# Latent attention: the order of evictions, query copies, weight splits and column sums in five queues

## The reference

```python
def rmsnorm(x, g):
    y = xf * lax.rsqrt(jnp.mean(xf * xf, axis=-1, keepdims=True) + EPS)
    return (y * g).astype(x.dtype)

mod = cond @ w_ada[i] + b_ada[i]                  # cond = silu(c); six vectors of 1024
sh1, sc1, gt1, sh2, sc2, gt2 = jnp.split(mod, 6, axis=-1)
h = rmsnorm(x, g_mix[i]) * (1.0 + sc1) + sh1

def mla(h, ...):
    cq = rmsnorm(h @ w_dq, g_q)                   # 1024 -> 384
    q = (cq @ w_uq).reshape(B, S, 8, 128 + 64)    # 8 heads; the last 64 are rotated
    ckv_kr = h @ w_dkv                            # 1024 -> 256 + 64
    ckv = rmsnorm(ckv_kr[..., :256], g_kv)
    k_rope = rope(ckv_kr[..., 256:], positions)
    kv = (ckv @ w_ukv).reshape(B, S, 8, 128 + 128)
    # causal softmax over 512 keys, p @ v, then o @ w_o
x = x + gt1 * mla(...)
...                                               # feed-forward, the second layer, the second block
```

## Time and profile before

| | us |
|---|---|
| median of 3 runs (2288.86 to 2292.99) | 2289.5 |
| the profiled execution | 2291.01 |
| its span | 2289.2 |
| TensorE busy in it | 2196.0 (96%) |
| VectorE, ScalarE, GpSimd busy | 1418.9, 964.0, 178.7 |

### The profile page before, as it was taken

How to read it: one execution, slowest core, us unless ns; L and a number is a source line. 1 busy time by engine, 2 the same in 40 slices (tenths; PEclk the granted TensorE clock), 3 DMA queues, 4 the chain that set the end, 5 groups by cost and what they waited for, 6 DMA issues and landing times.

```text
span 2289.2 us, 31979 instructions
## 1 busy us (share of the span) xinstructions
PE 2196.0 (96%) x13291; PEld 1940.5 (85%) x13291; DVE 1418.9 (62%) x2132; ACT 964.0 (42%) x1459; POOL 178.7 (8%) x155
## 2 busy tenths in 40 slices
PE   5988999999999899999989999999899999999998
PEld 3877888888898798898988999997778889899997
DVE  5676566556576667566446667654564545666674
ACT  3556343223256644463534444434443334443442
POOL 7210000000032100000010000002012001000000
PEclk8999999999999999999999999999999999999999
DMA  6442244555430212322312332333111332133230
GB/s 233 143 141 83 93 162 171 185 183 203 174 107 20 74 56 92 111 93 93 129 56 70 98 110 93 111 101 109 58 44 64 120 103 74 65 120 109 94 112 38
DMA packets 127734, 245.72 MB, mean 107 GB/s; under 512 B 4763, under 2 KB 36854, under 8 KB 127462
## 3 DMA queue, kind: packets, MB, share of 16 engines
q1 hardware_dynamic: 122832, 228.02, 29.5%
q0 software_dynamic: 4096, 15.28, 2.0%
q10 hardware_dynamic: 662, 0.37, 0.1%
HBM read 241.56 MB, written 2.10 MB: 106 GB/s over the span
## 4 chain that ended last, share of the span: by engine, by line
PE 81%; DVE 10%; ACT 4%; DMA 2%; issue 2%; POOL 0%; SPq 0%; DVEq 0%; ACTq 0%
PE PS L66 80%; DVE t L75 5%; ACT t L72 4%; DVE t L83 3%; DVE t L86 1%; DMA t<-in_ffn_w_dram 1%; PE PS L69 1%; DMA t<-in_w_ada_dram 1%; DVE t L79 1%; DMA t<-in_w_ff_dram 0%; DVE t L80 0%; DVE t L92 0%; POOL t L75 0%; DVE t L95 0%; DVE PS L75 0%
## 5 line engine op out<-in xcount | busy, mean ns | idle before, releaser
L66 PE MATMUL PS<-t,t 128*128 128x256 f32 (+4 forms) x12924 | 2145.4, 329 | 61.5 <-issue 14.2
L66 PEld LDWEIGHTS PS<-t,t 128*128 128x128 f32 (+2 forms) x12924 | 1896.5, 190 | 307.4 <-issue 72.7
L72 ACT ACTIVATE t<-t 128x512 f32<-128x512 f32 (+8 forms) x737 | 653.8, 904 | 947.4 <-DVE t L75 457.1
L75 DVE TENSOR_TENSOR t<-t,t 128x1024 fp32r<-128x1024 f32 (+9 forms) x692 | 777.9, 1141 | 387.8 <-ACT t L72 342.4
L72 ACT ACTIVATE t<-PS 128x512 f32<-128x512 f32 (+4 forms) x331 | 177.3, 550 | 245.2 <-PE PS L66 181.2
L75 POOL TENSOR_TENSOR t<-t,t 128x512 f32<-128x512 f32 (+2 forms) x71 | 87.5, 1233 | 1118.4 <-ACT t L72 949.6
L75 DVE TENSOR_TENSOR t<-t,PS 128x512 f32<-128x512 f32 (+2 forms) x134 | 83.2, 626 | 147.6 <-PE PS L66 141.4
L72 ACT ACTIVATE t<-t,t 128x256 fp32r<-128x256 f32 (+5 forms) x220 | 115.8, 536 | 92.2 <-DVE t L83 45.0
L83 DVE SCALAR_TENSOR_TENSOR t<-t,t,t 128x1024 f32<-128x1024 f32 (+2 forms) x157 | 145.2, 932 | 14.1 <-DMA t<-in_w_ada_dram 8.2
L83 DVE SCALAR_TENSOR_TENSOR t<-PS,t,t 128x512 f32<-128x512 f32 (+3 forms) x120 | 76.4, 642 | 99.2 <-PE PS L66 89.2
L69 PE MATMUL PS<-t,t 128*128 128x128 f32 (+1 forms) x367 | 59.7, 303 | 27.9 <-DVE t L79 6.7
(11 more groups left out here) (30 smaller groups left out, 154.3 us busy)
## 6 DMA issues: line engine op xcount, KB each, us to landing
t<-in_w_ff_dram SPq DMA_DIRECT2D x64, 1024.0 KB, 5.2
t<-in_ffn_w_dram SPq DMA_DIRECT2D x60, 1024.0 KB, 5.1
t<-in_w_ada_dram SPq DMA_DIRECT2D x36, 1024.0 KB, 5.8
t<-in_w_in_dram SPq DMA_DIRECT2D x13, 1024.0 KB, 5.2
t<-in_w_ada_dram POOLq DMA_DIRECT2D x24, 512.0 KB, 4.3
t<-in_swa_w_qkv_dram SPq DMA_DIRECT2D x6, 1024.0 KB, 5.6
t<-in_ffn_w_dram SPq DMA_DIRECT2D x8, 768.0 KB, 4.4
t<-in_w_in_dram SPq DMA_DIRECT2D x24, 256.0 KB, 3.7
```

Source lines behind the costliest of these rows:

```text
L66: return Instr(self.real and self.real.matmul(o, lhs, rhs, start=start, stop=stop, **more))
L72: return Instr(self.real and self.real.activation(o, src, func, **more))
L75: return Instr(self.real and self.real.tensor_tensor(o, a, b, op))
```

## The change

Instructions are moved within their queues; none is added or removed.

- In the first stage the split of dq's first weight goes in front of the row copies (ScalarE) and of the addition of the shift vector (VectorE).
- In dq, the split of dkv's first weight (`WX["dq"][0] + 2`) goes behind the evictions of the first token half (ScalarE) and behind the addition of their squares (VectorE). On TensorE the sums of the first half go from behind tile 1 of the second half's first weight to behind tile 0 of its second weight, the spread from there to behind tile 2.
- The copy of the rotated parts of heads 2 and 3 goes in front of the split in `act_uq`. That of heads 4 and 5 goes between the exponentials of heads 0 and 1, and on VectorE the softmax of head 1 goes in front of uq of heads 4 and 5.
- The column sums of vector 3 go, on TensorE, from behind the values of head 3 to behind those of head 5; on VectorE, from in front of the split of mo's first weight to behind the output of head 4.

```diff
@@ act_begin
             act_root(e, "n0", 1, D)
+            act_split(e, 0)
             e.wait_ge(acc, ("row", 7))
             for hf in range(2):
...
                 e.activation(TMP[s][0:1, :], PS[0:1, banks["row", hf], :], ACT.Copy).then_inc(copied, ("row", hf))
-            act_split(e, 0)
             act_normed(e, n0, 0, ALL)
@@ dve_begin
             dst = MOD[:, 0, 0:8]
+            dve_split(e, 0)
             e.wait_ge(acc, ("row", "t", 1))
             e.tensor_tensor(dst, PS[:, banks["row"], 0:8], dst, ALU.add).then_inc(mod, (0, 0))
-            dve_split(e, 0)
             dve_normed(e, n0, 0, ALL)
@@ act_uq
-        def act_uq(e, p, after0=None, lead=2):
+        def act_uq_copy(e, p):
+            act_rot_copy(e, ("qr", p), F, banks[("uq", p), 0, F], (("uq", p), 0, F), (part_lo, ("qr", 2 * p + 1)))
+
+        def act_uq(e, p, after0=None, lead=2, copied_before=False):
+            if p == 1:
+                act_uq_copy(e, p)
             act_split(e, WX["uq"][p] + lead)
             if after0:
                 after0()
-            act_rot_copy(e, ("qr", p), F, banks[("uq", p), 0, F], (("uq", p), 0, F), (part_lo, ("qr", 2 * p + 1)))
+            if p != 1 and not copied_before:
+                act_uq_copy(e, p)
@@ pe_mla_in
-                      mid={(1, 0, 1): lambda: pe_sums(e, "cq", 0, last=2), (1, 1, 0): lambda: pe_low_R(e, "cq", 0)})
+                      mid={(1, 1, 0): lambda: pe_sums(e, "cq", 0, last=2), (1, 1, 2): lambda: pe_low_R(e, "cq", 0)})
@@ act_mla_in
-                if hf == 0:
-                    act_split(e, WX["dq"][0] + 2)
-                else:
+                if hf:
                     act_root(e, "cq", 0, 384)
                 for n in range(3):
                     act_low_evac(e, "cq", n, hf, banks["dq", n, hf], ("dq", n, hf), sums0("n0"))
+                if hf == 0:
+                    act_split(e, WX["dq"][0] + 2)
@@ dve_mla_in
-                if hf == 0:
-                    dve_split(e, WX["dq"][0] + 2)
-                else:
+                if hf:
                     dve_diag(e, "cq", 0, place=DIAG[0][0])
                     dve_beside(e)
                 add_square(e, "cq", 1, hf)
+                if hf == 0:
+                    dve_split(e, WX["dq"][0] + 2)
@@ pe_mla
             pe_m_values(e, 3)
-            pe_columns(e, 0, 3, at=0)
             pe_m_turn(e, 5)
             pe_m_values(e, 4)
             pe_m_turn(e, 6)
             pe_m_values(e, 5)
+            pe_columns(e, 0, 3, at=0)
             pe_m_turn(e, 7)
@@ act_mla
             act_m_exps(e, 0)
+            act_uq_copy(e, 2)
             act_m_exps(e, 1)
             act_m_soft(e, 0)
-            act_uq(e, 2, lead=1)
+            act_uq(e, 2, lead=1, copied_before=True)
@@ dve_mla
             dve_m_soft(e, 0)
+            dve_m_soft(e, 1)
             dve_uq(e, 2, WX["uq"][2])
             dve_columns(e, 0, 4)
-            dve_m_soft(e, 1)
...
-            dve_columns(e, 0, 3)
             dve_split(e, WX["mo"][0])
             dve_m_soft(e, 6)
             dve_m_out(e, 3)
             dve_m_soft(e, 7)
             dve_m_out(e, 4)
+            dve_columns(e, 0, 3)
             dve_split(e, WX["mo"][1])
```

## The result

| | before | after |
|---|---|---|
| median, us | 2289.39 (2288.86 to 2292.99, 4 runs) | 2277.97 (2276.29 to 2278.55, 4 runs) |
| the profiled execution | 2291.01 | 2276.29 |
| its span | 2289.2 | 2274.5 |
| mean granted clock in it | 0.984 | 0.987 |

The ratio is 0.9947, with a 95% interval of 0.9935 to 0.996: faster, by 11.4 us in the medians (9.2 to 14.9 by the interval). The forecast was 2274.4 with a range of 2270.5 to 2281.5; the time lies inside, 3.6 us above the forecast. The spans of the two traces differ by more, 14.7 us, because the profiled execution of the changed kernel is the fastest of its four and that of before lies 1.6 above its median.

A forecast was written before the change was run, and what follows sets the result against it. TensorE, busy 96% of the span and working in program order, was taken as the bound, three long waits bringing low clock. Terms 1.4 + 4.8 + 2.1 + 1.4 + 5.4 = 15.1 us gave 2274.4 us, range 2270.5 to 2281.5.

The forecast's parts named there:

- The three long waits: TensorE waits of 3.14 (first sums of squares), 3.01 (rotation, queries 2 and 3) and 3.90 us (column sums, vector 3), beside low clock.
- the list of signs: Expected in the changed profile: long waits gone, TensorE's sum to 480 us 8 to 10 us smaller, clock 1.00 from 58 us.
- First split, 1.4: First stage: dq's first weight split in idle time beside the norm, whose first operation starts near 48.8, 1.4 us earlier.
- The lower bound: First split: the earlier norm meets another GpSimd operation, leaving a gain of about 0.1 us.
- Evictions in front of the split, 4.8: In dq: the 3.14 us wait before the sums of squares goes, and 1.65 us of low clock with it; 4.8 us.
- rival 4: ScalarE stuck at uq's split behind a late load, 2278.1 us if it takes 7.5; chance 0.05, plus 0.02 as a loss.
- Copy of queries 2 and 3, 2.1: Before ukv: TensorE gains 3.5 us with only 1 us of wait; 2.1 pass on, bounds 1.0 and 3.5.
- the load of `w_ada` as a cap: Before the first scores: VectorE's accumulation waits for this load, so only 2.1 of TensorE's 3.5 us pass on.
- rival 1: Waits go but the low clock stays, beside shorter idle pieces around 59, 120, 147 and 209 to 215; 2280.7 us, chance 0.17.
- Copy of queries 4 and 5 with the softmax, 1.4: Before the first turn: VectorE's chain loses its waits, not its work, softmax in idle time; 1.4 us, bounds 0.5 and 2.5.
- rival 2: VectorE paces the attention stage: the query parts give 0.5 to 1 instead of 3.5, the end 4; 2278.5 us, chance 0.12.
- Column sums, 5.4: Vector 3, last stage: the 3.90 us wait and low clock go, shorter waits remain; 5.4 us, bounds 2.3 and 6.5.

## Why the prediction was right, and where it was off

The direction, the size and the places were right; the forecast was 3.6 us too low. The two low stretches that the sum took to be gone cost 2.1 us at ukv and 1.5 behind the first turn in the changed kernel's trace, 3.6 together, and the kernel with the same order and extra products, whose clock stayed high there, had a median of 2274.99. Smaller misses of other terms, for and against, cancel beside that. By the prediction's own steps:

**What bounds the kernel.** The three long waits were the right places: with them 4.9, 2.5 and 5.9 us of the time go. All went from TensorE's list, as the list of signs said. The list's sum up to 480 us fell from 46.9 to 33.9 us, by 13.0 where 8 to 10 was forecast; 2.9 of it are loads in the first stage, which no edit touches. Two more signs did not come as written: the clock is not 1.00 from 58 us on, and of the 9.3 us by which the first turn is earlier (9 was the sign) 1.4 are the early load.

**First split, 1.4.** Held in direction, and in size as far as is known: 1.1 to 1.4 by the kernel without it, within a scatter of 1 to 2 us. The norm's first operation was put near 48.8 and stands at 47.51; against the small products that is 1.3 earlier, the rest is the earlier load. The lower bound, one more operation slowed by GpSimd, did not come. The contrary did: up to the second weight of dq three operations of the norm took 1.11, 0.98 and 1.26 us in before instead of 0.48, 1.9 us more in all, and in the changed kernel one took 0.74 and the two of this row 1.74 together, 1.1 more than usual in all:

```profile
54.31 1.74 DVE L83 SCALAR_TENSOR_TENSOR t<-t,t,t 128x256 fp32r<-128x256 f32 x2
```

That is 0.8 of the 1.0 us that this stretch gained over the 1.4.

**Evictions in front of the split, 4.8.** Held: 4.88 us in one pair of traces and 4.45 to 5.4 in the other, 3.14 of wait and its low clock; more, 6.45, where the low clock lasted 6.8 us. The cover of the load of uq held too; ScalarE waited for it 0.24 us and TensorE not at all, so rival 4 is out:

```profile
74.86 0.85 ACT L72 ACTIVATE t<-t 128x768 fp32r<-128x768 f32 x1 [0.24 <-DMA t<-in_mla_w_uq_dram]
```

**Copy of queries 2 and 3, 2.1.** One half of the mechanism was right: ukv waits for VectorE's low half, which is ready at 109.95 + 2.28 = 112.2, and starts at 112.33.

```profile
109.95 2.28 DVE L75 TENSOR_TENSOR t<-t,t 128x2048 fp32r<-128x2048 f32 x1
```

The other half, the load of `w_ada` as a cap, was not what set the size. With the clock high the distance from the second weight of dq to the first scores is 77.3 us in six kernels, and in two of them the first row maximum waits for TensorE last and not for the load; in the kernel with extra products at ukv alone:

```profile
138.75 0.29 DVE L86 CUSTOM_DVE_ANT_0 t<-PS,t 128x128 f32<-128x128 f32 x1 [0.39 <-PE PS L66]
```

So the copy is worth 2.5 us up to the scores, 1 us less than TensorE was to gain before the cap; the wait at ukv, 1.74 instead of 1, is most of that. The load came at another time in each execution, and where it was latest it took 0.55 and 0.9 us back before the first turn, in the others next to nothing. The 2.1 is thus near by size and in part by luck. The step that failed is "with only 1 us of wait": the wait was 1.74 us, and the sum took the clock to be high behind it. It fell, for 6.8 us, and the trace of the changed kernel kept 0.5 us of this term. That is rival 1 at this place. The argument that spoke against rival 1, a wait of 2.28 us at 59.7 that did nothing to the clock, was of a wait between wide products; here the 16 column sums stand in front of it. That such a wait is safe was itself too much to say: at that place thirteen profiles with waits of 0.68 to 2.43 us kept the clock, and the one with 2.76, the kernel with GpSimd's operation made short, lost it (TensorE's row, then the stretch):

```profile
60.01 53.88 PE L66 MATMUL PS<-t,t 128*128 128x256 f32 x370 [2.76 <-issue]
```

```profile
61.00:64.50 3.50, 3.50 (x19) 0.52 0.60 186
```

**Copy of queries 4 and 5 with the softmax, 1.4.** Here the step failed. "VectorE's chain loses its waits and not its work" holds for the copy, which alone gives 1.36. The softmax was put into idle time "after 157.3" at 1.05 us, and took 2.1, since GpSimd's product with the cosine starts 0.07 us ahead of it (149.39 and 149.46). The prediction weighed just this meeting for the norm, and not for the operation that it moved next to GpSimd's. The Trainium skill (SBUF — State Buffer, Who interferes with whom) says that `tensor_scalar` can take the port pair that VectorE shares with GpSimd, when its operands meet certain conditions, and that the later of the two is then blocked for the whole of the other's instruction. The trace agrees: 1.05 us longer beside 1.29, and 0.88 with the GpSimd operation at 0.20. Together the pair brought 0.3 us instead of 1.4. Behind the turn the clock was low, 1.5 us that the sum did not have; this is rival 1 at the turn and no price of the pair, as the kernel without the pair and the one with the copy alone lost the same there (19.30 and 19.34 against 17.73). So VectorE is what the turn waits for, as rival 2 has it, but through GpSimd; and the rest of rival 2, a last stage of only 4, did not come.

**Column sums, 5.4.** Held: 5.9 by the rows, 4.9 and 5.2 by the medians. The two waits that were put in its place, 1.0 for the scaling and 2.0 for softmax 6, measured 0.93 and 1.47 us. These two did not make the clock fall in any of the twelve profiles that have them; they stand behind transposes and wide products.

**The sum.** The terms as they came in the trace of the changed kernel: 1.4 + 5.3 + 0.3 - 1.5 + 5.9 = 11.4, against 15.1. The medians differ by 11.4 too, but that is no test of a tenth: each is good to about 1 to 2 us, and the two profiled executions carry 2.4 us more (the early load and the end of the span) that no edit made. The 1 us over the first split is for the most part the norm meeting GpSimd less; whether the change brought that was not settled, as the kernels with and without that step scatter by as much.

## What to carry to other kernels

Before an operation of VectorE is moved into idle time, look at what GpSimd does in that time: a free place in VectorE's own queue is not free while the two meet, and the price was most of the length of GpSimd's instruction (1.05 of 1.29 us). A wait of under 2 us in front of a long run of products can cost more than its length where TensorE did only small products before it; price it with the low clock as a case of its own, and where nothing else can fill it, products whose results nobody reads cost nothing that the rows show. And since the clock falls in one execution and not in the next, take such a term from several traces or from the mean clock of each run, never from one profile.

## What the runs showed of the hardware

The clock fell from 1.00 to 0.50 beside waits of 1.74 us (in front of ukv, in five of eight profiles that have this wait) and of 1.36 to 2.46 us (before the first turn, in eight of eleven profiles), each behind 16 products of one column, and was then low for 3.3 to 6.8 us. At the turn it fell in all five profiles with a wait of 2.45 or 2.46, and in three of the six with 1.36 to 1.41. With products of 128x512 ahead of the column sums it stayed at 1.00 in all three profiles at ukv (8 products) and in all three at the turn (8 or 5): six of six, against six of nineteen without. These products fill the wait as well, so the runs do not tell whether the idle time or the small products ahead of it are what counts. Its price is read from distances that agree to 0.06 us where the clock stays high (77.31 to 77.37 in six kernels up to the scores, 17.73 to 17.77 in six from the turn to the next mark): 1.1 to 2.1 us at ukv and 1.4 to 2.7 us at the turn, the upper values where it was low for 6.8 us and not 3.4. The Trainium skill (TensorE: Matmul & The Clock Gate, Part 1: The HAM clock gate) says that the number of slow products at the start of one kernel differs from run to run. The profiles show such differences in the middle of a kernel too, and in the runs they are 5 us of difference between executions of one kernel, going with 0.003 to 0.004 of mean clock. What exactly decides between two executions no run here shows.
